# Hybrid decoder trunk with grouped experts: H update moved on GpSimd, expert choice by ranks, norms and transposes by token tile, last expert pair taken out of the loop

## What is computed

```python
for i in range(DEPTH):                       # 4 layers
    y = mixer(h)                             # kind i % 3
    h = layer_norm(DN_ALPHA * h + y, ln_mix_g[i], ln_mix_b[i])
    m = grouped_moe(h, w_router, router_bias, e_w1[i], e_w3[i], e_w2[i])
    h = layer_norm(DN_ALPHA * h + m, ln_ffn_g[i], ln_ffn_b[i])

def grouped_moe(x, ...):
    scores = sigmoid(t @ w_router); sel = scores + router_bias
    best = argmax over groups of the sum of the group's two largest sel
    gates = scores of the two largest sel of that group, divided by their sum
    for e in range(16):
        out += gates[:, e:e+1] * ((silu(t @ w1[e]) * (t @ w3[e])) @ w2[e])
```

## Time and profile before

| what | value |
|---|---|
| median of 3 runs | 2234.33 us (2234.1 to 2235.07) |
| the profiled execution, its own time | 2229.25 us |
| its span, first to last instruction | 2227.4 us |
| TensorE busy | 1974.4 us (89%), granted clock 0.931 of full on average |
| VectorE, ScalarE, GpSimd busy | 754.7, 495.4, 158.7 us |
| the chain that ended last | PE 85%, DVE 10%, issue 3%, ACT 2%, DMA 1% |
| read from HBM | 501.8 MB |

### The profile page before, as it was taken

The page is one execution under the profiler, slowest core; times in us unless marked ns, Lnnn a source line. Parts: engine busy times, 40 slices in busy tenths (PEclk is TensorE's granted clock), DMA queues, the critical chain, the costliest instruction groups (busy, mean ns, idle before and its releaser), DMA issues.

```text
span 2227.4 us, 26152 instructions
## 1 busy us (share of the span) xinstructions
PE 1974.4 (89%) x9378; PEld 1139.9 (51%) x9379; DVE 754.7 (34%) x1568; ACT 495.4 (22%) x940; POOL 158.7 (7%) x96
## 2 busy tenths in 40 slices
PE   8989779999896669889989987899989988669997
PEld 7858644444573344343444535444458588444443
DVE  3435533233304442123322113233334255323324
ACT  1733201112203111011221101112225533111121
POOL 1110030000200030000020002000030100110000
PEclk9999979999896879889999997899999999889999
DMA  9330027999931138338994324679973300249994
GB/s 349 114 113 20 1 95 289 425 425 427 318 132 69 53 131 365 154 140 365 426 341 169 129 114 181 265 327 427 426 278 118 148 1 20 76 183 389 424 428 199
DMA packets 80016, 504.05 MB, mean 226 GB/s; under 512 B 7171, under 2 KB 11444, under 8 KB 55100
## 3 DMA queue, kind: packets, MB, share of 16 engines
q1 hardware_dynamic: 69808, 488.65, 54.5%
q0 software_dynamic: 2304, 8.39, 1.1%
q10 hardware_dynamic: 7820, 5.84, 0.9%
HBM read 501.80 MB, written 1.06 MB: 226 GB/s over the span
## 4 chain that ended last, share of the span: by engine, by line
PE 85%; DVE 10%; issue 3%; ACT 2%; DMA 1%; DVEq 0%; ACTq 0%; SPq 0%
PE bank L1687 22%; PE bank L1705 11%; PE bank L1409 10%; PE bank L1415 9%; PE bank L1678 7%; PE bank L1803 5%; PE bank L1435 4%; PE bank L1652 2%; PE bank L1517 1%; PE bank L1508 1%; PE bank L1751 1%; PE bank L1400 1%; PE bank L1698 1%; PE bank L1661 1%; PE bank L1522 1%
## 5 line engine op out<-in xcount | busy, mean ns | idle before, releaser
L1687 PE MATMUL bank<-ring,work 128*64 128x512 f32 x2176 | 485.7, 604 | 15.6 <-DVE work L1247 9.5
L1687 PEld LDWEIGHTS bank<-ring,work 128*64 128x64 f32 x2176 | 156.3, 139 | 336.1 <-issue 329.3
L1705 PE MATMUL bank<-ring,work 128*64 128x512 f32 x1088 | 242.3, 596 | 9.5 <-issue 4.9
L1409 PE MATMUL bank<-HT,ring 128*128 128x256 f32 x1024 | 232.9, 388 | 4.2 <-DMA ring<-in_a_w_in 2.3
L1409 PEld LDWEIGHTS bank<-HT,ring 128*128 128x128 f32 x1024 | 199.2, 195 | 42.4 <-issue 12.8
L1415 PE MATMUL bank<-ring,HT 128*128 128x512 f32 x448 | 193.3, 593 | 0.9 <-DVE HT L876 0.9
L1274 DVE TENSOR_TENSOR work<-bank,work 64x512 f32<-64x512 f32 x64 | 68.2, 1066 | 363.0 <-ACT work L808 363.0
L1678 PE MATMUL bank<-work 128*128 128x128 f32 x1152 | 156.4, 292 | 10.6 <-DVE work L1252 6.7
L1678 PEld LDWEIGHTS bank<-work 128*128 128x128 f32 x1152 | 143.1, 202 | 39.6 <-issue 30.3
L808 ACT ACTIVATE work<-bank 64x512 f32<-64x512 f32 x64 | 37.7, 589 | 520.9 <-PE bank L1687 520.9
L1242 DVE TENSOR_TENSOR work<-bank,lncols 128x512 f32<-128x512 f32 x72 | 49.8, 691 | 301.3 <-PE bank L1678 301.3
(11 more groups left out here) (283 smaller groups left out, 1995.9 us busy)
## 6 DMA issues: line engine op xcount, KB each, us to landing
ring<-in_e_w SPq DMA_DIRECT2D x192, 2048.0 KB, 13.0
ring<-in_a_w_in SPq DMA_DIRECT2D x16, 2048.0 KB, 16.1
ring<-in_c_w_in SPq DMA_DIRECT2D x8, 2048.0 KB, 14.8
ring<-in_b_w_in SPq DMA_DIRECT2D x6, 2048.0 KB, 17.0
ring<-in_a_w_out SPq DMA_DIRECT2D x4, 2048.0 KB, 7.8
ring<-in_c_w_out SPq DMA_DIRECT2D x4, 2048.0 KB, 7.8
ring<-in_b_w_out SPq DMA_DIRECT2D x2, 2048.0 KB, 8.8
gB<-in_ln_mix_g POOLq DMA_DIRECT2D x4, 512.0 KB, 3.9
```

Of the source, the lines that this page charges most:

```text
L1409: ins = mm(dst[:, 0:SEQ], wt[:, k, n * P:(n + 1) * P], HT[:, k, :], start=k == 0, stop=k == KC - 1)
L1687: ins = mm(bank[b][lo:lo + CAP, :], x[:, k, :], wt[:, k, :], start=k == 0, stop=k == KC - 1, skip_group_check=True)
L1705: ins = mm(bank[b][nh * CAP:(nh + 1) * CAP, :], h[:, m, :], w2[:, m, nh * 512:(nh + 1) * 512], start=m == 0, stop=m == 3, skip_group_check ...
```

## The change

**GpSimd.** The gain and shift rows are multiplied by alpha as soon as they have landed, and the third round over `H` goes. Behind a mixer's norm the update now waits until the first gather's second half has been shifted; VectorE's wait for it moves into each pass, behind `gather(0)`. **Expert choice.** Each score is compared with the three others of its group, and each group with the others; what has fewer than two (one) above it is chosen. The running count takes three products. **Norms.** Behind a mixer each tile is added, measured and normalised by itself, each normalisation in two halves with a signal each; behind the experts each block's statistics follow its last add. The refinement of the root takes four instructions instead of five. **Transposes** go tile by tile, and the next product waits for each copy singly. **First and last pair.** `up` waits for the second half of the gathered tokens only at its fifth block; the last pass stands outside the loop, written out once more on each engine, without gathers.

```diff
+        self.count = [c + n * passes - (b < 2) for b, (c, n) in enumerate(zip(self.count, per_pass))]
@@ SyncE: release of the last pass's sixth slot
+                    if (p, q) == (E // 2 - 1, 5):
+                        sp.wait_ge(filled[4], at[("moe", i)][4] + E // 2)
+                    else:
+                        sp.wait_ge(weights_read, (STEPS * (E // 2) - 1) * i + STEPS * p + FREED[q])
@@ GpSimd: residual
-                    own.wait()
+                    pool.wait_ge(h_ready, 2 + 2 * ph)
...
+                for row in (gB, bB):
+                    own.then(pool.tensor_scalar(row[:, :], row[:, :], ALPHA, None, ALU.mult))
+                own.wait()
...
-                    pool.wait_ge(xhat_ready, 2 * ph)
+                    pool.wait_ge(xhat_ready, 4 * ph)
+                    if with_moe:
+                        wait_copy(pool, "first", i, 1)
...
-                    own.then(pool.tensor_tensor(H[:, tt, :], H[:, tt, :], bB[:, :], ALU.add))
-                own.wait()
-                for tt in range(TT):
-                    pool.tensor_scalar(H[:, tt, :], H[:, tt, :], ALPHA, None, ALU.mult).then_inc(h_ready, 1)
+                    pool.tensor_tensor(H[:, tt, :], H[:, tt, :], bB[:, :], ALU.add).then_inc(h_ready, 1)
@@ VectorE: root, now of one tile or both
-                own.link(v.tensor_tensor(rs[:, 1, :], rs[:, 0, :], rs[:, 0, :], ALU.mult))
-                own.link(v.scalar_tensor_tensor(rs[:, 2, :], mv[:, :, 1], EPS, rs[:, 1, :], ALU.add, ALU.mult))
-                own.link(v.tensor_scalar(rs[:, 1, :], rs[:, 2, :], -0.5, 1.5, ALU.mult, ALU.add))
-                own.link(v.tensor_tensor(rs[:, 3, :], rs[:, 1, :], rs[:, 0, :], ALU.mult))
+                own.link(v.scalar_tensor_tensor(rs[:, 1, c], mv[:, c, 1], EPS, rs[:, 0, c], ALU.add, ALU.mult))
+                own.link(v.scalar_tensor_tensor(rs[:, 1, c], rs[:, 1, c], -0.5, rs[:, 0, c], ALU.mult, ALU.mult))
+                own.link(v.scalar_tensor_tensor(rs[:, 3, c], rs[:, 1, c], 1.5, rs[:, 0, c], ALU.add, ALU.mult))
+            def normalise(phase, tt):
+                for kh in range(2):
+                    dst = src = H[:, tt, kh * 512:(kh + 1) * 512]
...
+                    v.tensor_scalar(dst, src, mv[:, tt, 0:1], rs[:, 3, tt:tt + 1], ALU.subtract, ALU.mult).then_inc(xhat_ready, 1)
@@ VectorE: add_mixed
                         wait_copy(dve, "y", i, tt, nh)
                         block_stats(H, tt, nh)
+                        if nh:
+                            aggregate((tt,), 2)
+                            root((tt,))
+                            normalise(2 * i + 1, tt)
@@ VectorE: route, in place of first_max (three times), max and min
+                def ranks(x, sets, outp):
+                    n = sets * 4
...
+                    own.link(v.tensor_tensor(above, x4.unsqueeze(2).to_broadcast([P, sets, 4, 4]), x4.unsqueeze(3).to_broadcast([P, sets, 4, 4]), ALU.subtract))
+                    for w_, op in ((0, ALU.is_ge), (1, ALU.is_gt)):
...
+                        own.then(v.scalar_tensor_tensor(beaten[:, :, :, w_, :], above, 0.0, m, op, ALU.mult))
+                    own.wait()
+                    own.link(v.tensor_reduce(outp, pairs[:, 256:256 + n * 8].rearrange("p (n c) -> p n c", c=8), AX, ALU.add))
+                ranks(R[2], TT * GROUPS, R[3])
+                own.link(v.scalar_tensor_tensor(R[4], R[3], 2.0, R[2], ALU.is_lt, ALU.mult))
+                own.link(v.tensor_reduce(rg[:, 0, :], G4(4), AX, ALU.add))
+                ranks(rg[:, 0, :], TT, rg[:, 1, :])
+                own.link(v.tensor_scalar(rg[:, 2, :], rg[:, 1, :], 1.0, None, ALU.is_lt))
+                v.scalar_tensor_tensor(G4(7), G4(3), 2.0, rg[:, 2, :].unsqueeze(2).to_broadcast([P, TT * GROUPS, 4]), ALU.is_lt, ALU.mult).then_inc(mask_ready, 1)
@@ VectorE: experts
                 for g in range(2):
                     wait_data(dve, "first", i, g)
                     pair_x(g)
-                for g in range(2):
...
-                dve.wait_ge(h_ready, 2 * nres)
-                with dve.Fori(0, E // 2) as it:
+                def pair(it, final):
...
+                    if not final:
+                        dve.wait_ge(filled[0], it + (first[0] + 1))
+                        pair_x(0)
+                        dve.wait_ge(x_scaled, it * 2 + (E * i + 3))
+                        pair_x_shift(0)
+                    dve.wait_ge(h_ready, 2 * nres)
...
                         v.tensor_tensor(part(b), bank[b][:, :], part(b), ALU.add).then_inc(drained[b], 1)
+                        if final:
+                            dve.wait_ge(drained[b], first[b] + E // 2)
+                            block_stats(H, (b - 4) // 2, (b - 4) % 2)
+                with dve.Fori(0, E // 2 - 1) as it:
+                    pair(it, False)
+                pair(E // 2 - 1, True)
@@ TensorE (ScalarE's loop is split in the same way)
+                pss = [fill("ht", phase, k) for k in range(KC)]
+                for tt in range(TT):
+                    for k in range(KC):
+                        if phase and k % 4 == 0:
+                            pe.wait_ge(xhat_ready, 4 * (phase - 1) + 2 * tt + k // 4 + 1)
+                        ins = tr(pss[k][:, tt * P:(tt + 1) * P], src[:, tt, k * P:(k + 1) * P], ident)
...
+                    if phase is not None:
+                        wait_copy(pe, "ht", phase, k)
...
+                mm(ps[:, 0:2 * E], tri, rt[:, 7, :], start=True, stop=False, skip_group_check=True)
+                mm(ps[:, E:3 * E], ones[:, :], mask[0].unsqueeze(1).to_broadcast([P, 2, E]), start=False, stop=False, skip_group_check=True)
+                done(mm(ps[:, 2 * E:3 * E], ones[:, :], mask[1], start=False, stop=True, skip_group_check=True), "rank", i)
...
+                        if later is not None and k == KC // 2:
+                            later(1, 0)
...
-                    free(1, 0)
...
+                    if not final:
+                        head, tail = gather(1)
+                        head.then_inc(weights_read, 1)
+                        tail.then_inc(filled[1], 1)
...
+                with pe.Fori(0, E // 2 - 1) as it:
+                    pair(it, False)
+                pair(E // 2 - 1, True)
```

## The result

The changed kernel takes 2177.7 us (median of 4 runs, 2173.55 to 2182.84) against 2234.22 us (4 runs, 2228.72 to 2235.07): ratio 0.9753, 95% interval 0.9737 to 0.977. The profiled execution took 2173.55 us with a span of 2171.8, 55.6 less than the span before.

What follows compares the result with a forecast made beforehand. TensorE was busy for 89% of the span, with middle passes taken as fixed, so gains had to come between passes and mixers. The terms summed to -57.0 us against 2234.33, giving 2177 us, range 2155 to 2203.

Steps and rivals of the forecast that it cites:

- Norm and transposes: Behind each mixer: tile-by-tile norm starts tile 1 earlier and leaves 8 transposes; 4.4 us gained per seam.
- The clock in the seam: Router behind the mixer: clock stays high with no idle piece above 2 us; 2.2 us gained in layers 0, 2, 3.
- the clock stays low through the seams: Rival, chance 0.2: router 9.2 us worse, first `up` 1.5, ramps 2.4; total 2190 us.
- Expert choice: Between router and first gather: 15 linked instructions instead of 32 take 3.9 us; 18.5 us gained in all.
- The count in three products: Running count behind the expert choice: two of five products go; 0.85 us gained, four times, 3.4 in all.
- First `up`: Start of each layer's first pass: the wait for shifted tokens goes, 2.3 us four times; layer 1's first `up` 1.5 faster.
- H update: GpSimd's update, at most 11.5 us, moved beside the first `up`; VectorE needs it 15 us or more later; cost nothing.
- the row scaling: GpSimd's scaling of gain and shift rows beside the DeltaNet in layers 0 and 3: 1 us each lost, possible 0 to 5.5.
- Experts to mixer: Seam behind the experts, three times: 2.5 us each, 7.5 in all, plus 0.8 each, 2.4, from an earlier clock.
- The last pass: Written out behind the loop: two dropped gathers save 2.0 us a layer, first-visit code costs 4.0 (0.6 to 5.6); net +8.
- The worst rival: Last pass: 12 skipped `If` blocks on TensorE cost 2.36 us each, 28.3 a layer; total 2274 us; chance 0.04.
- Loads: Row loads, 1.05 MB, move into the busy ring: 2.5 us of transfer fits in 3.8 us of slack; cost nothing.

Runs made afterwards that it cites:

- the undo agrees: The kernel with TensorE's `up` overflow steps as one looped body and all eight passes in the loop, with the old joint norm and k-by-k transposes restored: 2176.64 us.
- the undo puts the ranks: The kernel with TensorE's `up` overflow steps as one looped body and all eight passes in the loop, with the old 32-instruction expert choice restored: 2169.97 us.
- the moved kernel: The changed kernel with 64 idle transposes at the head of TensorE's program, moving everything behind by 127 instructions: 2189.41 us, one run.
- the compact loop: The changed kernel with all eight passes in the loop, gathers kept, and TensorE's three `up` overflow blocks made one body in a loop: 2158.85 us.
- another program: The changed kernel with its written-out last pass, without gathers, also left without its overflow `If` blocks on all three engines: 2170.2 us.

## Why the prediction held, point by point

**The total** (2177 against 2177.7) held to 0.7 us by luck, with errors that cancel: the seams gave 4.0 us less than forecast, the last passes cost 5.6 more, the tails gave 2.7 less; against that, the mixers cost 1.4 less, and the first and overflow passes gave 9.5 us that no step had, 6.6 of them within the spread of one program.

- **Norm and transposes** came as worked out: 4.7 us against 4.4 (tile 1's transposes 3.64 us behind the mixer, forecast 3.45), and the undo agrees, 4.8 to 5.0 without the routers.
- **The clock in the seam** is the step that failed: "I take it to stay high", 2.2 us in three layers. The granted clock was 0.56 in the router of layer 0, behind idle pieces of 0.98 and 1.59 us. It gave 0.8, 1.3 and 0.7 (router 6.08, 5.6, 6.18; 6.85 before), which is nearly the whole shortfall of the seams. The rival "the clock stays low through the seams" came true for the router, but its other parts did not: layer 1's first `up` runs in 13.96 us, 1.6 less than before, and the tails are short.
- **Expert choice**: score to rank 3.93 us against 3.9; the undo puts the ranks at about 2.5 us and the missing holds at 1.4. The count in three products: 0.86 against 0.85. **First `up`**: 2.2 against 2.3.
- **H update**: "cost nothing" was right by 0.35 us. Beside it VectorE is held for 2.86, 2.91, 2.36 and 2.40 us, so its first product ends at 344.85 and the second `up` at 345.2. I had counted 15 us of cover. The mixers of layers 0 and 3 took 1.8 and 0.6 us more, forecast +1 each for the row scaling; four executions of the changed kernel spread over 1.2 and 1.4 us there, so its cost is small but not shown.
- **Experts to mixer**: 14.70 to 12.28, 2.4 us in each of three layers, forecast 2.5. Of the 2.4 of clock on top, the mixers behind show it in layer 1 at most (-3.0, against +1.1 in layer 2); in two further executions of the same program layer 1 gave only 1.0. The last norm gave 0.35, forecast 0.5.
- **The last pass** was right in sign and kind, wrong in both sizes: two gathers 0.98 instead of 2.0, the first visit 2.4 to 6.6, mean 4.4, instead of 4.0, with a bound of 5.6 that layer 1 passes. Net +3.4 a layer instead of +2.0. The worst rival (2.36 us at each of 12 blocks) is refuted: one to three stalls above 1 us stand in a last pass.
- **Loads**: middle passes are 29.44 throughout and no pass waits on the ring.

On fetching, the rows come first: "issue" stalls of 1.0 to 4.5 us stand on first visits, nearly all at jumps over `If` blocks (2.08 in the last pass above, 1.75 and 1.72 in the moved kernel), two at a loop's first jump back (1.71 and 1.17), a few of 1.0 to 2.1 us in straight code shortly behind a jump; none in the repeats, none in last passes without jumps. The queue's records show no packet in layer 0 from 370 to 540 us, where the loop repeats. The first half of the rule that I cited (the Trainium skill, "Runtime: NRT & Kernel Launch", section "Instruction fetch mechanics": a taken branch out of the fetched window waits for a fetch) agrees. Its preference for full unrolling does not hold where skipped `If` blocks are written out with the rest: the written-out last passes cost 13.6 us net of their saved gathers, and rolling the overflow steps up gained 17.4 (2176.22 to 2158.85). Where nothing is skipped it does no harm: 24.94 us a last pass.

By the Trainium skill, "SBUF — State Buffer", section "SBUF: two separate sides", GpSimd and a VectorE instruction in a two-port mode lock each other out of their shared port for a whole instruction. I had given this little weight. It fits what the rows show, 2.86 and 2.91 us beside GpSimd's two of 2.9, each ending with it; with the update early it is 3.2 us a layer on the path.

**Open**: why a given jump stalls. Layer 0's first pass took 30.0 us before and 36.2 after; one move by 127 instructions changed the pattern, and the length of the skipped code was never changed without its place. What decides whether the clock falls in the gap or in the router is not settled either. Not tried: the `down` steps' `If` blocks, and those of VectorE and ScalarE, made compact in the same way; and the compact loop with a last pass written out without them.

## What to carry to other kernels

Code that is jumped over can have a price at its first visit, here up to 7 us for a pass of 29: write rare cases as one body in a loop, compare the first repeat of a loop with the second, and look for "issue" at the jump before unrolling anything. When an idle gap is shortened, count the gap only, and not the clock: it can fall into the work behind it, and a gap of 1.1 us can cost more than the work that filled it. Move GpSimd's long instructions under work for which VectorE is not needed, and allow for VectorE standing still for the whole length of each.

## What the runs showed of the hardware that was not expected

- The same code, 127 instructions further on, takes 3.8 us longer in one pass (29.45 and 33.23), 3.5 of them in two stalls.
- Skipping a 2 us gather lengthened the pass by 0.7 us in three layers of four, by the clock: `down` 8.78 instead of 7.09 us behind a gap of 1.11. Behind a gap of 1.12 at the same place another program kept its clock in all four.
- Held VectorE instructions reach 2.91 us for one of 0.25, and only some are: the reciprocal above is not, and the one at 338.68 got in between two of GpSimd's.
- Executions of one and the same program differ by 9.5 us (2173.55 to 2183.03), mostly in the overflow passes; and one seam, layer 1's, is 22.5 or 24.1 us, with the router in 3.7 or 6.4.
